# Late input tiles of the second block in seven-product form, inside the attention stage

## The reference

```python
m = x @ w_in                                   # 1024 -> 7 * 1024 columns
q, k, v, xr, gr, gates = jnp.split(m, cuts, axis=-1)
ya = diff_attention(q, k, v, lambda_qk, subln_g, lam_init)
h = rg_lru(causal_conv(xr, conv_w, conv_b), gate_a_w, gate_a_b, gate_x_w, gate_x_b, lru_lambda)
yr = h * jax.nn.gelu(gr)
g = jax.nn.sigmoid(gates.reshape(B, S, N_BRANCH, D_MODEL))
merged = g[:, :, 0] * (ya @ w_br_attn) + g[:, :, 1] * (yr @ w_br_lru)
return merged @ w_out
```

## Time and profile before

| what | value |
|---|---|
| median of 3 runs | 3474.32 us (3473.58 to 3478.85) |
| the profiled execution, first to last instruction (its span) | 3468.5 us |
| PE busy | 3163.5 us (91%) |
| DVE busy | 2265.4 us (65%) |
| ACT busy | 723.2 us (21%) |
| POOL busy | 594.6 us (17%) |
| attention stage, layer 0 | about 1587 to 1720 us |
| attention stage, layer 1 | about 2565 to 2697 us |
| mean granted clock of TensorE | 0.96 of full speed |

### The profile page before, as it was taken

How to read it: one execution, slowest core, us unless ns; L and a number is a source line. 1 busy time by engine, 2 the same in 40 slices (tenths; PEclk the granted TensorE clock), 3 DMA queues, 4 the chain that set the end, 5 groups by cost and what they waited for, 6 DMA issues and landing times. The chain is left out here.

```text
span 3468.5 us, 55454 instructions
## 1 busy us (share of the span) xinstructions
PE 3163.5 (91%) x20794; PEld 2387.7 (69%) x20794; DVE 2265.4 (65%) x5755; ACT 723.2 (21%) x1783; POOL 594.6 (17%) x516
## 2 busy tenths in 40 slices
PE   8999889999999999999998988887899989888877
PEld 8996579999968979997885434343578864444433
DVE  8844648778576548772457777776634467777775
ACT  2101311111131211111322222222212322222222
POOL 0000000000000000000004544444100035444442
PEclk9999699999999989999999999999999999999998
DMA  5443014455312014452449999999734479999998
GB/s 203 161 161 121 1 67 163 160 174 183 134 61 87 4 63 170 162 218 85 158 164 407 421 422 422 422 421 421 303 124 158 194 288 421 421 422 422 422 421 330
DMA packets 116014, 829.18 MB, mean 239 GB/s; under 512 B 12784, under 2 KB 14320, under 8 KB 17424
## 3 DMA queue, kind: packets, MB, share of 16 engines
q0 software_dynamic: 73728, 536.90, 37.3%
q1 hardware_dynamic: 39488, 273.59, 21.3%
q10 hardware_dynamic: 2576, 15.59, 1.2%
HBM read 824.99 MB, written 1.05 MB: 238 GB/s over the span
## 5 line engine op out<-in xcount | busy, mean ns | idle before, releaser
L3194 PE MATMUL psum_all<-expert_rows,const_sb 128*128 128x512 f32 x2048 | 963.6, 628 | 189.0 <-ACT const_sb L3109 188.8
L2782 POOL DMA_INDIRECT expert_rows<-in_peer_uv_dram,head_experts x512 | 594.4, 1161 | 2831.1 <-issue 1911.2
L3194 PEld LDWEIGHTS psum_all<-expert_rows,const_sb 128*128 128x128 f32 x2048 | 403.1, 201 | 731.8 <-issue 465.9
L2934 DVE CUSTOM_DVE_ANT_0 expert_rows<-expert_rows,xn 128x1024 f32<-128x1024 f32 x512 | 616.5, 1223 | 256.3 <-DMA expert_rows<-in_peer_uv_dram,head_experts 252.3
L2457 PE MATMUL psum_all<-x,weight_ring 128*128 128x256 f32 x1024 | 228.6, 381 | 0.0
L3109 ACT ACTIVATE const_sb<-cst,head_weights 128x128 f32<-128x128 f32 x496 | 158.6, 390 | 329.4 <-DVE head_weights L2945 326.0
L409 PE MATMUL psum_all<-xn,weight_ring 128*128 128x136 f32 (+1 forms) x1408 | 193.1, 281 | 20.6 <-DMA weight_ring<-in_ffn_in_dram 9.6
L2457 PEld LDWEIGHTS psum_all<-x,weight_ring 128*128 128x128 f32 x1024 | 192.3, 191 | 28.2 <-issue 3.5
L409 PEld LDWEIGHTS psum_all<-xn,weight_ring 128*128 128x128 f32 x1408 | 176.7, 193 | 22.1 <-issue 9.8
L409 PE MATMUL psum_all<-xn,weight_sums 128*128 128x136 f32 (+1 forms) x1056 | 142.6, 278 | 0.6 <-DVEq L641 0.6
L3105 ACT ACTIVATE dots<-dots 128x4 f32<-128x4 f32 x124 | 25.5, 205 | 559.5 <-DVE dots L2934 559.4
(11 more groups left out here) (617 smaller groups left out, 5099.5 us busy)
## 6 DMA issues: line engine op xcount, KB each, us to landing
weight_ring<-in_ffn_in_dram SPq DMA_DIRECT2D x88, 1024.0 KB, 4.8
weight_ring<-in_w_in_dram SPq DMA_DIRECT2D x48, 1024.0 KB, 4.8
weight_ring<-in_ffn_out_dram SPq DMA_DIRECT2D x32, 1024.0 KB, 4.8
weight_ring<-in_ffn_out_dram SPq DMA_DIRECT2D x16, 768.0 KB, 4.2
weight_ring<-in_hyb_in_dram SPq DMA_DIRECT2D x12, 1024.0 KB, 4.8
weight_ring<-in_peer_q_dram SPq DMA_DIRECT2D x12, 1024.0 KB, 15.6
expert_rows<-in_w_v_dram ACTq DMA_DIRECT2D x8, 1024.0 KB, 5.9
weight_ring<-in_br_attn_dram SPq DMA_DIRECT2D x8, 1024.0 KB, 7.0
```

The lines of the kernel that those rows point to most:

```text
L2782: pool.indirect_dma_start(out=rows[:, j, :], out_offset=None, in_=a["peer_uv"], in_offset=bass.IndirectOffsetOnAxis(ap=idx[:, n, j:j + 1], ...
L2934: dve.tensor_tensor_reduce(row, row, xt[:, n, :], 1.0, 0.0, ALU.mult, ALU.add, dots[:, n, j:j + 1]).then_inc(S.dotted, 1)
L3194: mm = pe.matmul(sums(n, half), diag[:, j, :], rows[:, j, D + half * 512:D + (half + 1) * 512], start=False, stop=last and j == TOPK - 1)
```

## The change

The 16 late tile pairs are made in the seven-product form too. Per pair PE issues 7 products of 4 blocks on 128 tokens each (`late_begin`: products 1 to 4, `late_onto`: 5 and 6 onto the banks of 1 and 2, `late_end`: 7 onto the bank of 4). The four banks (6, 7, 2, 3, `late_quad`) are one set, reused by every pair; for that the scores keep only banks 0 and 1, one buffer instead of two, and `score(u)` waits until unit u-1's scores have been read. POOL makes the four weight sums per pair, double-buffered by pair. The input sums are those of the query/key stage; in layer 0, where they were made of the unnormalized input, DVE makes them again from h at that stage's end. ACT copies products 1 and 2 and takes the first tile's low half; DVE adds the parts and takes the other three quarters. DVE's order within a unit changes: last pair's takes, last unit's attention output, `weigh(u)`, parts of pair 2u, `add(u+1)`, takes of pair 2u, the two convs (units 2 to 5), parts of pair 2u+1. ACT's exponentials run one unit ahead. SP loads three slots deep. The last product of the last pair comes after the head sums, which use bank 4 instead of 6.

```diff
+                                for n in range(4):
+                                    step(dve.tensor_tensor(tin[:, n], *input_pair(x_late, n), ALU.subtract))
...
-                    sc = lambda u: psum_all[:, (u % 2) * 1024:(u % 2 + 1) * 1024].rearrange("p (c k) -> p c k", c=4)
+                    sc = psum_all[:, 0:1024].rearrange("p (c k) -> p c k", c=4)
...
+                    late_quad = [psum[b][:, 0:HALF] for b in (6, 7, 2, 3)]
...
+                        @block.gpsimd
+                        def _(pool):
+                            for t in range(LATE):
+                                wt, ws = late_raw(t), wsum[:, t % 2]
+                                pool.wait_ge(*late_landed(S, t))
+                                if t >= 2:
+                                    pool.wait_ge(S.products, PRODUCTS * (t - 1))
+                                pool.tensor_tensor(ws[:, 0], wt[:, 1, :, 0, :], wt[:, 1, :, 1, :], ALU.add).then_inc(S.weight_sums, 1)
+                                pool.wait_ge(S.weight_sums, 4 * t + 1)
+                                pool.tensor_tensor(ws[:, 1], ws[:, 0], wt[:, 0, :, 0, :], ALU.subtract).then_inc(S.weight_sums, 1)
+                                pool.tensor_tensor(ws[:, 2], wt[:, 0, :, 0, :], wt[:, 1, :, 0, :], ALU.subtract).then_inc(S.weight_sums, 1)
+                                pool.wait_ge(S.weight_sums, 4 * t + 2)
+                                pool.tensor_tensor(ws[:, 3], wt[:, 0, :, 1, :], ws[:, 1], ALU.subtract).then_inc(S.weight_sums, 1)
...
+                            def late_begin(t):
+                                pe.wait_ge(*late_landed(S, t))
+                                if t:
+                                    pe.wait_ge(S.low_taken, t)
+                                product(bank[0], lambda j: wt[:, 0, j, 0, :], lambda j: x_late[:, j, 0, lo])
+                                pe.wait_ge(S.weight_sums, 4 * t + 1)
+                                if t:
+                                    pe.wait_ge(S.taken, 2 * t - 1)
+                                product(bank[1], lambda j: ws[:, 0, j, :], lambda j: tin[:, 0, j, :])
+                                pe.wait_ge(S.weight_sums, 4 * t + 2)
+                                if t:
+                                    pe.wait_ge(S.second, t)
+                                product(bank[2], lambda j: ws[:, 1, j, :], lambda j: tin[:, 1, j, :])
+                                pe.wait_ge(S.weight_sums, 4 * t + 3)
+                                if t:
+                                    pe.wait_ge(S.taken, 2 * t)
+                                product(bank[3], lambda j: ws[:, 2, j, :], lambda j: tin[:, 2, j, :])
+                            def late_onto(t):
+                                pe.wait_ge(S.copied, 2 * t + 1)
+                                product(bank[0], lambda j: wt[:, 0, j, 1, :], lambda j: x_late[:, j, 1, lo], onto=True)
+                                pe.wait_ge(S.copied, 2 * t + 2)
+                                pe.wait_ge(S.weight_sums, 4 * t + 4)
+                                product(bank[1], lambda j: ws[:, 3, j, :], lambda j: x_late[:, j, 1, hi], onto=True)
+                            def late_end(t):
+                                pe.wait_ge(S.third, t + 1)
+                                product(bank[3], lambda j: wt[:, 1, j, 1, :], lambda j: tin[:, 3, j, :], onto=True)
...
                             def score(u):
-                                if u >= 2:
-                                    pe.wait_ge(S.added, u - 1)
+                                if u:
+                                    pe.wait_ge(S.added, u)
...
                             for u, (hp, n) in enumerate(units):
                                 if u + 1 < len(units):
                                     score(u + 1)
-                                late_product(per_unit * u)
+                                late_begin(2 * u)
+                                late_onto(2 * u)
+                                late_end(2 * u)
                                 pe.wait_ge(S.probs, u + 1)
...
+                            def late_parts(t):
+                                dve.wait_ge(S.products, PRODUCTS * t + 3)
+                                dve.wait_ge(S.copied, 2 * t + 1)
+                                dve.tensor_tensor(part[:, U2, b, :], part[:, P1, b, :], bank[2], ALU.add).then_inc(S.second, 1)
+                                dve.wait_ge(S.products, PRODUCTS * t + 4)
+                                dve.wait_ge(S.second, t + 1)
+                                dve.tensor_tensor(part[:, U3, b, :], part[:, U2, b, :], bank[3], ALU.add).then_inc(S.third, 1)
+                            def late_take(t):
+                                dve.wait_ge(S.products, PRODUCTS * t + 6)
+                                dve.tensor_tensor(z1[:, hi], part[:, U2, b, :], bank[1], ALU.add).then_inc(S.taken, 1)
+                                dve.wait_ge(S.third, t + 1)
+                                dve.wait_ge(S.copied, 2 * t + 2)
+                                dve.tensor_tensor(z2[:, hi], part[:, U3, b, :], part[:, P5, b, :], ALU.add).then_inc(S.fourth, 1)
+                                dve.wait_ge(S.products, PRODUCTS * t + 7)
+                                dve.tensor_tensor(z2[:, lo], part[:, U2, b, :], bank[3], ALU.add).then_inc(S.taken, 1)
...
+                            add(0)
+                            for u in range(len(units)):
+                                if u:
+                                    late_take(2 * u - 1)
+                                    take_out(u - 1)
+                                weigh(u)
+                                late_parts(2 * u)
+                                if u + 1 < len(units):
+                                    add(u + 1)
+                                late_take(2 * u)
                                 if 2 <= u < 6:
                                     conv(2 * u - 4)
                                     conv(2 * u - 3)
+                                late_parts(2 * u + 1)
+                            take_out(len(units) - 1)
+                            late_take(LATE - 1)
...
-                            last_late = per_unit * len(units) - 1
-                            late_part(last_late, 0, range(4, KD))
-                            pe.wait_ge(S.late_read, last_late)
+                            late_onto(LATE - 1)
+                            pe.wait_ge(S.turned_in, len(units))
                             pe.wait_ge(S.o_squares, len(units))
-                            head_sums(pe, cst, z[:, 0:AH, PADC:], AH, 1, banks[6], S.o_sums)
-                            late_part(last_late, 1, range(KD)).then_inc(S.late_ready, 1)
+                            head_sums(pe, cst, z[:, 0:AH, PADC:], AH, 1, banks[4], S.o_sums)
+                            late_end(LATE - 1)
```

129 lines of the change are left out of this document (79 added, 50 removed).

## The result

The changed kernel takes 3508.14 us (median of 4 runs, 3500.58 to 3521.93), the kernel before on the same chip 3476.59 us (3473.58 to 3482.24); ratio 1.0094, 95% interval 1.0073 to 1.0115: some 33 us slower (25 to 40). The forecast was 3490 us: the direction was right, the loss was about twice the predicted 15.4 us, and the time lies above the range. The profiled execution took 3500.58 us and spans 3498.8 us, 30.3 more than before's 3468.5.

A forecast was written before the change was run, and what follows sets the result against it. TensorE was taken to bound the attention stages; -13.6 us from the form, +28 of stalls and +1 for weigh gave +15.4 on 3474.3, forecast 3490 us, range 3458 to 3500.

The forecast's parts named there:

- The form's gain: Late pairs on TensorE: 6.25 us instead of 6.80, 1.10 saved per unit; with both edges 6.8 us per layer, 13.6 in all.
- A sum on GpSimd: Each 128 x 512 weight sum on GpSimd takes 1.16 us, a pair's four 4.8 us with a small gap.
- Held VectorE, eight stalls: Units 2 to 5, both layers: GpSimd's sums hold VectorE's two-input operations, TensorE stalls 3.5 us each time, 28 us in all.
- the alternation: Unit 2: VectorE's z2 take and chained conv operations take turns with GpSimd's sums; parts end at 16.1, wanted at 12.6 us.
- The scaling of weigh: VectorE's weigh: scalings likely among the held operations; weigh held by two sums costs 0.1 to 0.2 us, 1 us in all.
- Rival 1: VectorE isn't held, only GpSimd is; the 13.6 us gain stays, 3461 us; chance 0.27.
- rival 2: VectorE is held, but GpSimd's sum takes only 0.69 us: eight stalls of 1.6 us, about 3474 us; chance 0.14.
- 3: GpSimd becomes the bound, from 1.78 us per sum on; at 2.1 us 3506 us or more; chance 0.05.
- rival 4: Late pairs save nothing because weight loads set the pace: 6.80 us again, 17.6 us more; chance 0.04 including anything unseen.
- The start: Attention stage's start: one score buffer makes score(1) wait for add(0), so the first late product starts 1.2 us later.
- The end of the stage: Last unit: head scales no longer covered, one product (0.89 us) behind the head sums; a gain of 0.3 us per layer taken.
- The clock: TensorE behind stalls: half speed may cost about 1.7 us each, none to 14 for eight; nothing summed, 10 us in range.

The follow-up runs named there:

- the cut sums: Changed kernel with GpSimd's four sums per pair cut to four elements each, every wait kept: ratio 0.9990 to the kernel before, stages 125.5 and 123.9 us.
- The filled kernel: Changed kernel plus useless TensorE products: seven before the seventh product of pair 2u+1 in units 2 to 5, five behind the stage's last product; ratio 1.0059 to before.

## Why the prediction was right in its direction and wrong in its size

- **The form's gain: right, a little low.** A pair in the attention stage takes 1599.83 - 1593.58 = 6.25 us, as in the earlier trace rows. With nothing held a stage was predicted at 131.8 - 6.8 = 125.0; the cut sums gave 125.5 and, at a whole clock, 123.9. A unit saved 1.3 us there and not 1.10 (15.33 to 14.01).
- **A sum on GpSimd: near.** 1.27 to 1.32 us by line, not 1.16; the four of a set take 5.4 instead of 4.8 us when they meet VectorE.
- **Held VectorE, eight stalls: right, a little less each.** The four stalls are 3.06, 3.07, 2.85 and 3.28 us in layer 0 and 3.07, 3.46, 2.86 and 2.95 in layer 1, 24.6 us against the 28. The place (third part, units 2 to 5) and the alternation are as written. That four operations are held is right, which four is not: I had the z2 high take held and the first conv operation free. In units 2 to 4 of layer 0 the take got ahead of the sums (0.28 us), and the conv's first operation, with one tensor input, was held in its place (1.23 to 1.33 us against 0.41); in unit 5 both were held. That the price came out so near is in this part luck. The scaling of weigh (L2631), called likely, is held, and so is an operation on 128x2 (L2629, 950 ns against 228), which I had left out. Rival 1 falls; rival 2 and 3 had the wrong duration of a sum; rival 4 falls by the first point.
- **The start: its length right, its clock left out.** Score(1) waits 1.0 us for the add, and the first late product starts 1.2 us later, as written. The clock behind it (0.83 over the first 10 us) costs about 1.6 us a stage, by the two layers of the cut sums.
- **The end of the stage: priced a little too well in itself.** I took a gain of 0.3 us. The idle time ahead of the gate stage went from 0.94 to 2.70, since only 0.9 us of products stand behind the head sums; the last unit, from its first product to the gate stage, takes 20.44 us before and with the cut sums alike, so nothing is gained. What I missed is the clock behind the gap, in the gate stage.
- **With the waits filled** a stage takes 142.4 us, where the terms without a clock gave 139.5 (125.0, 14 of stalls, 0.5 of weigh). By the rows of layer 0, against the 123.9: the fillers with the waits left beside them are 13.4, the other waits for VectorE 2.1 (half of it in unit 7), and the first pair behind the start at a lower clock 1.6 (its second to fourth product took 3.94 us in place of 2.68). About 1 us is spread in tenths.
- **The clock: the step that failed.** "I put nothing of it in the sum and 10 us in the range." The filled kernel, with nearly the same waits of VectorE (13.4 us a stage in place of 12.3), is at 1.0059, +20.5 us (14 to 27), within which the 15.4 of the sum lie; the changed kernel is at 1.0094, +33. The 12 us between (2 to 22) are what falls when the gaps are there: about 7 in the two stages (146.8 + 144.7 - 142.3 - 142.5 = 6.7) and the rest, by the averages above some 3 us each, at the starts of the gate stages, where I looked for none. The clock behind the stage's start, about 1.6 us a stage, is in both kernels and comes on top. So the term that I put at nothing comes to 12 us by the two ratios, or about 15 with the starts, and the range held 10 for it. The row for it was in my hand: the earlier trace rows had 0.57 over 4 us behind 2.98 us of idle time, and the working priced eight stalls up to 14 us. With stalls forecast longer than that row's idle time, most of that belonged in the sum.

Left open: of the 7.4 us behind the stages in the profiled execution 1.6 lie ahead of the first gather (0.3 in layer 0, 1.3 in layer 1, where the clock was 0.91) and 6.6 in the stretch of the gathers (630.5 and 631.3 us against 625.3 and 629.9), less 0.8 behind it. Over all executions that stretch scatters between 624 and 631 us, so these 6.6 us aren't shown to come from the change.

## What to carry to other kernels

Price an idle gap of TensorE twice: once for its length, and once for the clock behind it, here 12 us beside 24.6 us of stalls, and look for gaps at stage boundaries, both where a faster tail uncovers one at the end and where a single buffer opens one at the start. Elementwise work with two inputs on GpSimd isn't free help for VectorE: beside it VectorE's three conv steps took 4.27 us instead of 1.53. In this kernel such sums cost least on VectorE itself (0.69 against 1.27 us each, 9 us less in the two stages with the convs in the same places); on GpSimd they did least harm where VectorE had nothing long to do. If a reordering only moves the wait, draw where the other engine's work starts and ends, and place the long operations in its gaps.

## What the runs showed of the hardware that I had not expected

- VectorE's operations on 128x2 elements took 950 ns on average beside GpSimd's sums (at most 1310) and 228 ns alone: one tiny operation waits as long for a sum as a large one does.
- Memsets of 128x512 on GpSimd (0.53 us each) leave VectorE's conv steps at 0.48 us but stretch its 128x4 operation from 170 to 297 ns; copies (0.64 us each) stretch three conv steps from 1.53 to 1.98.
- Two idle times of 1.26 and 1.02 us with 0.7 us of scores between them were followed by a lower clock in sixteen of eighteen stage starts; with one more product between them in none of two.
- Useless products made a kernel no slower, and by the medians faster: 3456.53 against 3464.18 us with ten of them, five a layer (the intervals of the ratios overlap).
